# Gating of tiles 1 to 4 behind the attention, one buffer for sample values, and a reordered output projection in a one-core decoder step

## The reference, cut to what matters

```python
h = rmsnorm(xp, attn_norm[l])
u, vn, q, k, v = mix_projection(h, w_in[l], ln_v_g[l], ln_v_b[l], pos_p)
a_out = gmlp_chunk_prompt(u, vn, w_s[l], b_s[l])        # u * (tril(w_s) @ vn + b_s), chunks of 128
res = [dilated_branch_prompt(q, k, v, w, r) for (w, r) in DILATED]
b_out = combine_branches([o for o, _ in res], [s for _, s in res])
xp = xp + jnp.concatenate([a_out, b_out], axis=-1) @ w_out[l]
xp = xp + peer_ffn(rmsnorm(xp, ffn_norm[l]), peer_w_q[l], peer_sub_keys[l], peer_u[l], peer_v[l])
# peer_ffn: q = x @ w_q; top 16 of 128 x 128 keys in each of 8 heads;
#   hid = gelu(u_tab[eid] . x);  y = sum of g * hid * v_tab[eid]
```

## Time and profile before

| | |
|---|---|
| median of 3 runs | 1680.44 us (1676.32 to 1685.04) |
| profiled execution | 1688.18 us, span 1686.4 us |
| busy | PE 1396.6 us (83%), DVE 1084.1 (64%), ACT 634.9 (38%), POOL 653.7 (39%) |
| moved | 664.81 MB, 394 GB/s over the span |
| chain that ended last | DMA 47%, PE 26%, DVE 12%, issue 10%, ACT 5% |
| second projection | about 118 to 258 us |
| attention of tiles 1 to 4 | about 262 to 420 us |
| output projection to key scores | about 420 to 600 us |
| expert stage of tiles 1 to 4 | about 600 to 1686 us |

### The profile page before, as it was taken

One profiled execution on the slowest core, in us unless ns is written; L12 is line 12 of the kernel. 1 busy time (PEld: TensorE's weight loads), 2 busy tenths in 40 slices (PEclk: granted clock), 3 DMA queues, 4 the chain that ended last, 5 costly groups with the idle time before them and its releaser, 6 DMA issues.

```text
span 1686.4 us, 17753 instructions
## 1 busy us (share of the span) xinstructions
PE 1396.6 (83%) x5164; PEld 617.7 (37%) x5164; DVE 1084.1 (64%) x2884; ACT 634.9 (38%) x1889; POOL 653.7 (39%) x703
## 2 busy tenths in 40 slices
PE   8999995868999988888877877777777777777776
PEld 5585663435334433343322322222222222222211
DVE  1459988968000156777766766666668888888654
ACT  1421113546211044444444544444445444444443
POOL 3034333323467643333343333333333333333331
PEclk9999997889899999999999999999999999999999
DMA  9798899999999999999999999999999999999996
GB/s 344 307 355 324 311 329 399 394 404 392 357 379 403 410 405 418 408 417 403 399 420 421 421 421 422 422 421 422 421 421 421 421 422 421 407 421 407 421 398 257
DMA packets 112144, 664.81 MB, mean 394 GB/s; under 512 B 13072, under 2 KB 14336, under 8 KB 52400
## 3 DMA queue, kind: packets, MB, share of 16 engines
q0 software_dynamic: 97824, 571.75, 83.9%
q1 hardware_dynamic: 14224, 91.93, 13.9%
HBM read 658.03 MB, written 5.60 MB: 394 GB/s over the span
## 4 chain that ended last, share of the span: by engine, by line
DMA 47%; PE 26%; DVE 12%; issue 10%; ACT 5%; POOL 1%; DVEq 0%; ACTq 0%; SPq 0%; POOLq 0%
DMA area_r<-in_uv_tab,eid 30%; DMA area_w<-in_uv_tab,eid 13%; PE bank L920 7%; PE bank L909 4%; PE bank L640 4%; PE bank L864 2%; PE bank L811 2%; ACT area_c L1016 2%; DVE area_r L1707 2%; PE bank L571 1%; DMA area_r<-in_uv_tab,eidT 1%; DVE area_x L1724 1%; DVE area_r L1716 1%; PE bank L780 1%; DMA area_w<-in_w_in 1%
## 5 line engine op out<-in xcount | busy, mean ns | idle before, releaser
L1886 POOL DMA_INDIRECT area_r<-in_uv_tab,eid x436 | 414.6, 951 | 747.1 <-PE bank L920 414.4
L920 PE MATMUL bank<-area_r,area_c 128*128 128x512 f32 (+1 forms) x1152 | 560.5, 617 | 156.0 <-ACT area_c L1016 155.9
L1716 DVE CUSTOM_DVE_ANT_0 area_r<-area_r,bank 128x1024 f32<-128x1024 f32 x308 | 375.0, 1218 | 215.3 <-DMA area_r<-in_uv_tab,eid 215.1
L920 PEld LDWEIGHTS bank<-area_r,area_c 128*128 128x128 f32 (+1 forms) x1152 | 198.4, 188 | 511.2 <-issue 510.5
L1266 ACT ACTIVATE area_c<-hid 128x1 f32<-128x1 f32 x416 | 84.2, 202 | 537.2 <-DVE hid L1716 536.4
L920 PE MATMUL bank<-area_w,area_c 128*128 128x512 f32 (+1 forms) x432 | 214.5, 624 | 63.1 <-ACT area_c L1016 63.0
L1716 DVE CUSTOM_DVE_ANT_0 area_w<-area_w,bank 128x1024 f32<-128x1024 f32 x108 | 131.3, 1217 | 70.7 <-DMA area_w<-in_uv_tab,eid 70.5
L1707 DVE CUSTOM_DVE_ANT_0 area_r<-area_r,bank 128x1024 f32<-128x1024 f32 x128 | 152.8, 1211 | 32.5 <-DMA area_r<-in_uv_tab,eid 32.2
L1886 POOL DMA_INDIRECT area_w<-in_uv_tab,eid x108 | 102.0, 944 | 173.6 <-PE bank L920 169.8
L640 PE MATMUL bank<-area_w,area_t 128*128 128x384 f32 (+1 forms) x448 | 157.7, 509 | 3.2 <-DMA area_w<-in_w_in 2.6
L1016 ACT ACTIVATE area_c<-ident,area_c 128x128 f32<-128x128 f32 x364 | 146.1, 401 | 34.9 <-ACT area_c L1016 1.1
(11 more groups left out here) (204 smaller groups left out, 1315.8 us busy)
## 6 DMA issues: line engine op xcount, KB each, us to landing
area_w<-in_w_in SPq DMA_DIRECT2D x12, 1536.0 KB, 10.6
area_w<-in_k_cache SPq DMA_DIRECT2D x8, 1920.0 KB, 13.9
area_w<-in_w_q SPq DMA_DIRECT2D x14, 1024.0 KB, 8.8
area_w<-in_w_out SPq DMA_DIRECT2D x4, 2048.0 KB, 14.6
area_w<-in_v_cache SPq DMA_DIRECT2D x4, 1920.0 KB, 10.8
area_r<-in_uv_tab,eid POOLq DMA_INDIRECT x436, 16.8
area_v<-in_v_cache SPq DMA_DIRECT2D x4, 1152.0 KB, 7.7
area_x<-in_x_p SPq DMA_DIRECT2D x6, 512.0 KB, 15.1
```

The costliest lines, as they stand in the source:

```text
L920: mm = pe.matmul(acc[0:n, c, :], diag[by_pe(i) % DG][:, 0:n], x_ring[s][:, D + c * 512:D + (c + 1) * 512], start=(i == 0), stop=False, ski ...
L1716: vec.tensor_tensor_reduce(out=u, in0=u, in1=x_cur, scale=1.0, scalar=0.0, op0=ALU.mult, op1=ALU.add, accum_out=hid[t % 2][:, j:j + 1]).th ...
L1886: nc.gpsimd.indirect_dma_start(out=ring[s], out_offset=None, in_=table, in_offset=bass.IndirectOffsetOnAxis(ap=where, axis=0)).then_inc(la ...
```

## The change

Five things, all in one edit:

- The normalisation, mixing and gating of tiles 1 to 4 leave the second projection. DVE normalises the four tiles after its last dot of tile 0 and gates them then; PE mixes tiles 1 and 2 ahead of the last PV, tiles 3 and 4 among the first products of the output projection. `mix_psum` puts them into other PSUM halves.
- Since `u_tok` and `vn` now live through the attention, `vc_odd` goes: all eight samples' values use one place, and SP loads those of b+1 when PV of b is done. The other half of `w_out`, the first `w_q` pieces and the store of the samples' `vn` move back in SP's order; x of tile 1 comes ahead of them.
- 84 instead of 75 dots by the end of the projection (`DOTS_PROJ`), `ROUTE_PROJ` one or two units earlier, and one dot instead of two ahead of a sample.
- `project_out` takes the attention's k blocks 2 to 7 first and the gated blocks 0 and 1 last. For tile 1 it is written out: eight v rows are weighed before x is added.
- DVE clears `wd` in place of ACT, and GpSimd's v gathers 6 to 11 wait for `pv_done` itself.

```diff
-DOTS_FIRST, DOTS_PROJ = 12, 75
-ROUTE_PROJ = {1: 2, 7: 3, 13: 4, 20: 5}
+DOTS_FIRST, DOTS_PROJ = 12, 84
+ROUTE_PROJ = {1: 2, 6: 3, 12: 4, 18: 5}
...
-        vc_even = cut(area_w, 0, CK // P, DB)
-        vc_odd = [cut(area_v, NT * DB, VC_SPLIT, DB), cut(area_c, 1408, CK // P - VC_SPLIT, DB)]
+        vc = cut(area_w, 0, CK // P, DB)
...
-            return 2 if before else 0
+            return 1 if before else 0
...
             for b in range(NB):
                 sp.wait_ge(scored, samp_at[b] + 1)
                 if b + 2 < NB:
                     load_kc(b + 2)
                 elif b == NB - 2:
                     load_w_o_cols(0)
+                sp.wait_ge(pv_done, samp_at[b] + 1)
+                if b + 1 < NB:
+                    load_vc(b + 1)
                 else:
-                    sp.wait_ge(route_link, HEADS * LINKS)
-                    for h in range(3):
-                        load_wq(wq_ring[h], h, wq_again[h])
-                sp.wait_ge(pv_done, samp_at[b] + 1)
-                if b + 2 < NB:
-                    load_vc(b + 2)
-                elif b == NB - 2:
                     load_w_o_cols(1)
+            sp.wait_ge(p_turned, len(ATT))
+            load_x(1)
             sp.wait_ge(pv_done, len(ATT))
...
-            for t in range(1, NT):
+            for t in range(2, NT):
                 load_x(t)
+            sp.wait_ge(route_link, HEADS * LINKS)
+            for h in range(3):
+                load_wq(wq_ring[h], h, wq_again[h])
...
                     for u in group(i - 1):
                         turn_probs(u)
+                    if i == hi + 1:
+                        mix(1)
+                        mix(2)
                     if group(i - 2):
                         outputs(group(i - 2))
...
+            OUT_K = list(range(2, KD)) + [0, 1]
...
-            for t in range(1, NT):
-                turn_gated(t)
             pe.wait_ge(qkT_ready, len(QK))
-            pe.wait_ge(gT_ready, NT)
             pe.wait_ge(proj_read, len(UNITS))
             attend(NG0, NG)
             pe.wait_ge(att_ready, len(ATT))
             pe.wait_ge(w_out_again[0], 16)
-            project_out(1, 0)
+            out_products(1, 0, OUT_K[:3])
+            mix(3)
+            mix(4)
+            out_products(1, 0, OUT_K[3:6])
+            turn_gated(1)
+            turn_gated(2)
             turn_weights()
+            pe.wait_ge(gT_ready, 2)
+            out_products(1, 0, OUT_K[6:])
             start_sum(0)
             pe.wait_ge(wd_ready, 1)
+            weigh_first(8)
+            out_residual(1, 0)
+            turn_gated(3)
+            turn_gated(4)
             pe.wait_ge(w_out_again[1], 16)
             project_out(1, 1, 4)
...
             gelu()
-            act.wait_ge(pv_done, len(ATT))
-            act.wait_ge(v_out, 16 * (NT + 1))
-            act.wait_ge(masked, len(ATT))
-            for g in range(GROUPS):
-                clear(g)
+            for t in (1, 2):
+                copy_gT(t)
             copy_weights()
+            act.wait_ge(v_out, 16 * NT)
+            for t in (3, 4):
+                copy_gT(t)
...
             dots_to(SLOTS)
-            dve.wait_ge(pv_done, len(ATT))
-            dve.sem_inc(v_free, VR)
+            for t in range(1, NT):
+                ln_apply(t)
+            for t in range(1, NT):
+                gate_u(t)
             weights()
+            for g in range(GROUPS):
+                vec.memset(wd[g], 0.0).then_inc(wz, 1)
```

More of the change, by code:

```diff
@@ L171, in build @@
         lnst = cut(area_c, 3288, NT * 8)
-        wd = [cut(area_c, g * D, D) for g in range(3)] + [cut(area_v, (NT - 1) * D, D)]
+        wd = [cut(area_c, g * D, D) for g in range(3)] + [cut(area_v, NT * D, D)]
         diag = [cut(area_c, s * P, P) for s in range(DG)]
@@ L281, in build, with mix_psum @@
         NQ0 = 4
-        MIX_AT = {0: 4} | {t: NC + 14 + 2 * (t - 1) for t in range(1, NT)}
+        MIX_AT = {0: 4}
         STATS_AT = {0: 0} | {t: NC + t - 1 for t in range(1, NT)}
-        APPLY_AT = {t: STATS_AT[t] + (2 if t == 0 else 5) for t in range(NT)}
+        APPLY_AT = {0: STATS_AT[0] + 2}
+        def mix_psum(t):
+            return half(6) if t == 0 else half(t % 2)
         ROTATE_AT, TURN_AT = {}, {}
@@ L645, in turn_gated @@
                 n = TILES[t][1]
-                pe.wait_ge(gated, 1 if t == 0 else NT)
+                pe.wait_ge(gated, t + 1)
                 if t >= 2:
@@ L962, in _ @@
                     turn_qk(i)
-                for t in range(1, NT):
-                    if u == MIX_AT[t]:
-                        mix(t)
-            for t in range(1, NT):
-                turn_gated(t)
             pe.wait_ge(qkT_ready, len(QK))
-            pe.wait_ge(gT_ready, NT)
             pe.wait_ge(proj_read, len(UNITS))
@@ L1256, in copy_weights @@
                 for g in range(GROUPS):
-                    ins = copy(wd[g][:, 0:D:CG + 1], half(7)[:, CG * g:CG * (g + 1)])
+                    ins = copy(wd[g][:, 0:D:CG + 1], half(5)[:, CG * g:CG * (g + 1)])
                 ins.then_inc(wd_ready, 1)
@@ L1340, in _ @@
                     copy_qkT(i)
-            for t in range(1, NT):
-                copy_gT(t)
-            def clear(g):
-                copy(wd[g].rearrange("p (a b) -> p a b", a=KD), ident[:].unsqueeze(1).to_broadcast([P, KD, P]), 0.0).then_inc(wz, 1)
             act.wait_ge(qz, 2)
@@ L1482, in gate_u @@
                 b0 = 0 if t < SAMP else GA
-                out = half(6 + t % 2)[0:n, 0:DA]
+                out = mix_psum(t)[0:n, 0:DA]
                 ps = out.rearrange("p (g d) -> p g d", g=GA)
```

80 lines of the change are left out of this document (34 added, 46 removed).

## The result

The changed kernel takes 1693.68 us (median of 8 runs, 1690.66 to 1700.15), the kernel before beside it 1682.18 (8 runs). The ratio is 1.0063, 95% interval 1.0043 to 1.0083: it is slower by some 10.6 us, where 1672 was forecast with a range from 1662 to 1686. The profiled execution of the changed kernel took 1690.66 us (span 1688.9), its fastest run, and that of before, 1688.18, was slower than any of the 8 runs beside it (up to 1685.47); so the two traces are only 2.5 us apart. Besides, two kernels with the same program up to 420 us reach the first PV of a sample at 294.7 and at 300.2 us. So a trace is used here to say where time goes and what waits for what, and the ratios, each from runs taken in turn with the kernel before, to say how much.

A forecast was written before the change was run, and what follows sets the result against it. The prediction took transfers to bound the kernel, with gains only from idle transfer time in the first 480 us. Its terms, 10 - 8.5 + 7.0 = 8.5 us, took the median of 1680.44 to 1672 us, range 1662 to 1686.

The forecast's parts named there:

- the end can only come earlier if the transfer engines lose less in the first 480 us: Whole kernel: expert-row fetches run at about 421 GB/s from slice 22 on, so only earlier idle transfer time can be won.
- From 600 us on nothing differs but the shift: Expert stage from 600 us: claimed to run as before, only moved in time by what was gained earlier.
- First term: Second projection, 130 to 246 us: nine more dots' gathers fill idle transfer time, plus 10 us, bounds 6 and 12.8.
- the sign by which the text itself would be wrong: Second projection: DVE's dots there waiting for rows by more than 5 us.
- Second term: Attention, 262 to 415 us: 10.5 us shorter but 10 us idle instead of 1.5, minus 8.5 us, bounds minus 1 and minus 15.
- the floor of 13.8 us: Attention: no cycle from one PV to the next shorter than about 13.8 us: PV 2.9, value load 10.8, and the issue.
- Third term: From the attention to 484 us: early weights and rows fill 7.0 of 7.8 idle us, bounds 3 and 7.8.
- the sign of being right: Behind the attention: DVE's chain of normalisations, gates and memsets taking under 20 us.
- if this chain were 5 us longer, the eight rows would still be early: Behind the attention: DVE's 14.3 us chain has slack before the first weighed row; beyond 7 us it costs the excess.
- C: Attention: value loads as slow as key loads, 13.9 us, cycle floor 16.9 us, 24 us idle; 1686 us, chance 0.13.
- the four: Whole kernel: the forecast 1672 us (0.50), gain given back 1679 (0.17), slow value loads 1686 (0.13), quick ones 1667 (0.20).
- four mixes and four turns: Second projection: PE loses some 3 us of work, which only starts the saturated attention a little sooner; counted as nothing.

The follow-up runs named there:

- e13: The kernel before with x of tile 1 asked for ahead of x of the other tiles and the first three w_q pieces: 1682.5 us, ratio 0.9989.
- e3: The changed kernel with the first half of w_out loaded behind the last sample's values instead of ahead: 1694.8 us, ratio 1.0062 to the kernel before.

## Why the prediction was wrong

**The frame.** The step that failed is the first: "the end can only come earlier if the transfer engines lose less in the first 480 us". It was read off a page that shows the transfers busy everywhere from slice 22 on the earlier trace rows. But between the two long stretches of transfers stands one point that only PE and DVE can release, the first added slot, and six slots are all the lead that can be carried over it. Before, GpSimd waited 7.2 us there with the rows still on their way and DVE waited 1.36 us for the first: both bounds stood within 2 us of each other. A term in transfer time could therefore win 2 to 4 us (an estimate from these waits and the constants), while a term in PE's time moves that point itself. The change was counted in the first unit and paid for in the second. "From 600 us on nothing differs but the shift" is the same error, and the hole at 620 us shows it. In its own unit the sum came to 2.5 us by 600 us (1.0 MB), not 8.5, so even that lead was overestimated.

**First term, nine dots: +10 forecast.** The share rose by 0.03 of the 0.11 that were free (0.92, where near 1 was expected), the rate to 345 GB/s where 355 was expected, and the sign by which the text itself would be wrong, over 5 us of waiting for rows, came: 6.4 us up to 262 us and another 8.6 to 274. That the load of DVE stays level was right, but it stayed level by moving dots in front of the first mask. Measured: 0 to 6 us lost.

**Second term, the attention: -8.5 forecast.** Its size in idle transfer time was right, 10.7 us from 262 to 415 us where 10 were counted, but that was partly luck, for the stage was to be 142.5 us long. The landing was right, 10.7 us where 10.8 was taken. The attention was to be 10.5 us shorter, and from first mask to last PV it is 148.2 us against 149.5. The cycles sum to 109.7 us where 104.1 were counted: the three long ones to 48.6, as planned (48.9), the four short ones (14.6, 14.7, 13.8, 18.0) to 61.1 against 55.2. Most of that is the last, 18.0, behind the w_out load, which the floor of 13.8 us left out. Behind the cycles come another 5.8 us where the prediction had "about 1 us": the mixes on PE and the lower clock. By ratio the one place alone cost 12 us, and 8 with w_out late and x first. An estimate from the Trainium skill's round robin between queues ("DMA: Bandwidth & Descriptors", section "Queues, rings and completion order") has a value load land after 9.9 us whatever stands in GpSimd's queue. The median was 10.7, so the row was the better guide, and the load that stood behind a 2 MB load on its own queue took 14.9; the estimate leaves out what stands ahead on the same queue.

**Third term, the pocket: +7.0 forecast.** In transfer time nearly right: 393 GB/s, which is 5.4 us back of the 7.0, and no window under 330 behind the first row. The first row was weighed 8.7 us closer to the attention's end where 7 was said; the DVE chain was shorter than its 14.3 us in work (memset 0.91, not 1.1), but waited 13.9 us for mixes: from the last dot (408.7 us) to the end of the last memset (436.4) it is 27.8 us, where under 20 was the sign of being right. The first row was weighed at 437.9 and not near 434. Measured as a part, the rows ahead cost 4 to 8 us. The sentence "if this chain were 5 us longer, the eight rows would still be early" asked when the rows come and never what they push back on PE, or that they had been nearly free where they stood, beside DVE's routing.

**The rivals.** C, slower by the one value buffer, had the right part and the wrong mechanism: it decided from 13.1 us of landing, and the landing was not slow. None of the four had the time of PE as its unit, and none gave 1694.

**What held.** The order of loads with x first removed the wait for x, though alone it gave no time that can be told (e13). That PE loses "four mixes and four turns" in the projection was put at nothing. That was too low: together with DVE's part and the rest of the bundle it is the gain of some 10 us.

## What to carry to other kernels

Before a gain is counted in idle time of the transfer engines, find the points where a consumer hands back the first slot of a new stage; a lead longer than the slots is lost there, and only the way of the engines to that point counts. Work that runs in the shadow of another engine's serial piece is nearly free, and moving it forward to feed the transfers puts it on the way. A change made of several parts can hide its one gain: here undoing two small parts and changing one load's place turned 0.6% slower into 0.2% faster, the latter only just clear of noise.

## What the runs showed of the hardware

- A load of 1920 KB issued 11.4 us behind one of 2048 KB on the same queue landed after 14.9 us; the median of all eight of 1920 KB was 10.7, the lowest 10.1. With the 2048 KB behind it instead (e3), the longest of the eight landed after 11.1 us.
- Behind a wait of 5.2 us PE's granted clock was 0.50, the lower level, and stayed there up to 428 us while PE worked. The first three windows:

```profile
404.00:408.00 4.00, 0.00 (x0) 0.00 (x0) 3.93 (x11) 1.58 (x5) 0.00 (x0) 0.94 0.62 265
408.00:412.00 4.00, 3.21 (x24) 1.69 (x27) 3.75 (x12) 0.00 (x0) 3.00 (x3) 0.50 0.47 129
412.00:416.00 4.00, 2.98 (x19) 1.10 (x14) 2.45 (x7) 0.99 (x3) 3.09 (x4) 0.50 0.90 294
```

- A DVE memset of 128 x 1024 float32 took 0.91 us, and two such stand 1.07 us apart.
